# First weight block behind each norm: products with upper parts first, from a zeroed bank

## The reference, cut to what matters

```
def rms_norm(x, g):                      # first model
    y = xf * rsqrt(mean(xf * xf) + 1e-6)
    return y * g
h = rmsnorm(x, ln1_g[l]) * (1.0 + sc1) + sh1     # second model, modulated
z = h @ w_in[l]
...
h = rmsnorm(x, ln2_g[l]) * (1.0 + sc2) + sh2
f = (silu(h @ w_gate) * (h @ w_up)) @ w_down
```

## Time and profile before

| | |
|---|---|
| time, median of 3 runs | 2083.06 us (2082.49 to 2087.9) |
| the profiled execution, its own time | 2090.85 us |
| its span, first to last instruction | 2089.0 us |
| PE busy | 2033.1 us, 97% of the span, 12394 products |
| DVE busy | 1717.8 us, 82% |
| ACT busy | 1248.3 us, 60% |
| mean granted TensorE clock | 0.986 of full speed |
| up to the mixture of experts | some 1220 us of the span |

### The profile page before, as it was taken

How to read it: one execution, slowest core, us unless ns; L and a number is a source line. 1 busy time by engine, 2 the same in 40 slices (tenths; PEclk the granted TensorE clock), 3 DMA queues, 4 the chain that set the end, 5 groups by cost and what they waited for, 6 DMA issues and landing times. The chain is left out here.

```text
span 2089.0 us, 31399 instructions
## 1 busy us (share of the span) xinstructions
PE 2033.1 (97%) x12394; PEld 1760.4 (84%) x12395; DVE 1717.8 (82%) x1984; ACT 1248.3 (60%) x1258; POOL 49.0 (2%) x84
## 2 busy tenths in 40 slices
PE   9999999999899999999999999999999999999998
PEld 8889996987799989799998878888888788888876
DVE  6868887786788878778788788988898889989997
ACT  5664444542443455643345767777777777777775
POOL 0000001000000000000000000000000000000000
PEclk9999999998899999999999999999999999999999
DMA  7358861301477735388874259998999899999995
GB/s 284 126 199 287 307 231 54 112 15 48 167 279 263 259 127 181 107 307 302 302 262 147 101 198 374 355 377 327 377 349 370 322 366 359 358 352 364 358 352 207
DMA packets 79466, 534.53 MB, mean 256 GB/s; under 512 B 11840, under 2 KB 13120, under 8 KB 15584
## 3 DMA queue, kind: packets, MB, share of 16 engines
q1 hardware_dynamic: 71744, 481.04, 62.1%
q0 software_dynamic: 7440, 51.49, 6.8%
q10 hardware_dynamic: 144, 0.02, 0.0%
HBM read 531.47 MB, written 1.05 MB: 255 GB/s over the span
## 5 line engine op out<-in xcount | busy, mean ns | idle before, releaser
L2433 DVE TENSOR_TENSOR weights_lo<-ring,weights_hi 128x2048 fp32r<-128x2048 f32 x193 | 436.8, 2280 | 63.7 <-ACT weights_hi L2427 63.4
L826 PE MATMUL bank<-acts_hi,weights_hi 128*128 128x256 f32 x1584 | 454.1, 287 | 6.9 <-DVE acts_lo L425 4.3
L403 DVE TENSOR_TENSOR weights_lo<-ring,weights_hi 128x2048 fp32r<-128x2048 f32 x161 | 368.1, 2290 | 110.0 <-ACT weights_hi L393 108.9
L393 ACT CAST weights_hi<-ring 128x2048 fp32r<-128x2048 f32 x161 | 306.9, 1908 | 250.1 <-PE bank L826 224.6
L826 PE MATMUL bank<-acts_lo,weights_hi 128*128 128x256 f32 x1584 | 448.1, 283 | 0.0
L826 PE MATMUL bank<-acts_hi,weights_lo 128*128 128x256 f32 x1584 | 448.0, 283 | 0.0
L2427 ACT CAST weights_hi<-ring 128x2048 fp32r<-128x2048 f32 x192 | 367.4, 1918 | 80.5 <-PE bank L2948 49.9
L826 PEld LDWEIGHTS bank<-acts_hi,weights_hi 128*128 128x128 f32 x1584 | 303.6, 192 | 15.9 <-issue 12.9
L2948 PE MATMUL bank<-weights_hi,xg_hi 128*128 128x512 f32 x768 | 305.2, 397 | 6.7 <-issue 2.9
L826 PEld LDWEIGHTS bank<-acts_lo,weights_hi 128*128 128x128 f32 x1584 | 303.8, 192 | 2.6 <-issue 1.4
L826 PEld LDWEIGHTS bank<-acts_hi,weights_lo 128*128 128x128 f32 x1584 | 303.7, 192 | 0.0
(11 more groups left out here) (498 smaller groups left out, 2868.7 us busy)
## 6 DMA issues: line engine op xcount, KB each, us to landing
ring<-in_experts SPq DMA_DIRECT2D x192, 1024.0 KB, 6.6
ring<-in_dense SPq DMA_DIRECT2D x162, 1024.0 KB, 4.9
ring_more<-in_experts SPq DMA_DIRECT2D x96, 1024.0 KB, 6.7
ada<-in_ada POOLq DMA_DIRECT2D x48, 1024.0 KB, 5.1
silu_c<-in_c SPq DMA_DIRECT2D x3, 512.0 KB, 6.9
resid<-in_x SPq DMA_DIRECT2D x2, 512.0 KB, 4.2
out<-resid SPq DMA_DIRECT2D x4, 256.0 KB, 2.2
small<-in_consts SPq DMA_DIRECT2D x1, 649.5 KB, 10.3
```

Source lines behind the costliest of these rows:

```text
L393: nc.scalar.copy(split[0][:, n % SPLITS, :], ring[:, n % RING, :]).then_inc(hi_ready, 1)
L403: nc.vector.tensor_tensor(split[1][:, n % SPLITS, :], ring[:, n % RING, :], split[0][:, n % SPLITS, :].bitcast(F32), ALU.subtract).then_in ...
L826: ins = nc.tensor.matmul(bank[:, f * T:(f + 1) * T], split[w][:, m % SPLITS, k * 256 + f * P:k * 256 + (f + 1) * P], acts[x][:, k, :], sta ...
L2433: ins = nc.vector.tensor_tensor(split[1][:, at, lo:hi], place(j)[0][:, lo:hi], split[0][:, at, lo:hi].bitcast(F32), ALU.subtract)
```

## The change

It has four parts.

1. A new function, `to_features_upper_first`, takes the place of `to_features` for the first block at six places: gate block 0 of FFN 0, 1 and 2, the receptance block `q` = 4, and `win(0)` of both mixers. It first multiplies a piece of the table that holds zeros with 512 columns into the whole bank, which starts the sum, and then makes the same 48 products in another order: those with upper parts of a pair (8) wait for `at_hi`, those with its lower part (4) for `at_lo`, in the order upper 0, upper 1, lower 0, upper 2, lower 1, upper 3, lower 2, lower 3.
2. The block's bank is now 7 instead of 0, at the five norms, as DVE still reads banks 0 to 3 when the products begin; whoever reads the result reads bank 7.
3. In a modulated norm ACT writes the upper part of pair 0 straight from the bank, without `AT`, and makes the full value of pair 2 as well; DVE makes that of pair 3 and then that of pair 0, which only the lower part needs now.
4. The two filling products behind the transposes are left out ahead of mixer 0, FFN 2 and mixer 1.

```
             def act_columns(self, act):
-                for b in range(4 if self.direct else 2):
+                at_once = range(4) if self.direct else (0,) if self.parts else ()
+                for b in range(4 if self.direct else 3 if self.parts else 2):
                     act.wait_ge(turned, 4 * self.turns + b + 1)
...
-                        dst = acts[0] if self.direct else AT
+                        dst = acts[0] if b in at_once else AT
...
-                    for c in range(2, 4):
-                        at_round(act, self.no, c)
+                    at_round(act, self.no, 3)
...
             def dve_columns(self, dve):
                 if not self.direct:
-                    for b in range(2, 4):
+                    for b in (3, 0) if self.parts else (2, 3):
                         dve.wait_ge(turned, 4 * self.turns + b + 1)
+                        if b == 0:
+                            dve.wait_ge(at_hi, 4 * self.no + 1)
...
+                        if c == 0:
+                            dve.wait_ge(at_ready[0], self.no + 1 - skipped[0])
                         at_rest(dve, self.no, c)
...
+        def to_features_upper_first(pe, m, bank, no):
+
+            def product(f, k, w, x, stop):
+                return nc.tensor.matmul(bank[:, f * T:(f + 1) * T],
+                                        split[w][:, m % SPLITS, k * 256 + f * P:k * 256 + (f + 1) * P],
+                                        acts[x][:, k, :], start=False, stop=stop)
+
+            def upper(c):
+                pe.wait_ge(at_hi, 4 * no + c + 1)
+                for f in range(2):
+                    for k in (2 * c, 2 * c + 1):
+                        for w in range(2):
+                            product(f, k, w, 0, False)
+
+            def lower(c):
+                pe.wait_ge(at_lo, 4 * no + c + 1)
+                for f in range(2):
+                    for k in (2 * c, 2 * c + 1):
+                        ins = product(f, k, 0, 1, f + k == KT)
+                return ins
+
+            nc.tensor.matmul(bank, const("causal", P, P), const("cos", 0, 2 * T), start=True, stop=False)
+            landed(pe, m)
+            upper(0)
+            upper(1)
+            lower(0)
+            upper(2)
+            lower(1)
+            upper(3)
+            lower(2)
+            lower(3).then_inc(used, 1)
...
-                                to_features(pe, at["gate", j], pb[j % 2], None if j else no)
+                                if j:
+                                    to_features(pe, at["gate", j], pb[j % 2])
+                                else:
+                                    to_features_upper_first(pe, at["gate", 0], pb[7][:], no)
...
-                        norm.pe(pe, *((2, 3), (6, 2), (3, 2))[name])
+                        norm.pe(pe, *((2, 3), (6, 0), (3, 0))[name])
...
+                        elif q == 4:
+                            to_features_upper_first(pe, nk + q, pb[q % 4][:], numbers[1])
...
+                            if i == 0:
+                                to_features_upper_first(pe, n0, pb[7][:], no)
...
-                        norm.pe(pe, *((2, 2), (4, 1))[l])
+                        norm.pe(pe, *((2, 0), (4, 1))[l])
```

More of the change, by code:

```diff
@@ L515, in act_columns @@
                         f = 2 * b + i
-                        dst = acts[0] if self.direct else AT
+                        dst = acts[0] if b in at_once else AT
                         ins = nc.scalar.activation(dst[:, f, :], pb[b][:, i * T:(i + 1) * T], ACT.Identity,
                                                    scale=self.gain(f), bias=self.bias(f) if self.bias else 0.0)
-                    if self.direct:
+                    if b in at_once:
                         ins.then_inc(at_hi, 1)
@@ L1406, in _ @@
                             act.wait_ge(used, at["gate", j] + 1)
+                            gate_bank = pb[j % 2 if j else 7]
                             if conv is None:
@@ L1409, in _ @@
                                     act.wait_ge(hidden, hb + j - 1)
-                                nc.scalar.activation(sg[:, j % 2, :], pb[j % 2][:], ACT.Silu).then_inc(gate_copied, 1)
+                                nc.scalar.activation(sg[:, j % 2, :], gate_bank[:], ACT.Silu).then_inc(gate_copied, 1)
                             else:
@@ L1415, in _ @@
                                     act.wait_ge(gate_pads, 2 * conv + 2)
-                                nc.scalar.copy(gp[:, j % 2, :, 2:], pb[j % 2][:].rearrange("p (f t) -> p f t", f=2)).then_inc(gate_copied, 1)
+                                nc.scalar.copy(gp[:, j % 2, :, 2:], gate_bank[:].rearrange("p (f t) -> p f t", f=2)).then_inc(gate_copied, 1)
                             round_to(act, at["up", j] + 4)
@@ L1671, in _ @@
                             to_tokens(pe, nk + q, pb[q % 4])
+                        elif q == 4:
+                            to_features_upper_first(pe, nk + q, pb[q % 4][:], numbers[1])
                         else:
-                            to_features(pe, nk + q, pb[q % 4], None if q % 4 else numbers[q // 4])
+                            to_features(pe, nk + q, pb[q % 4], None if q else numbers[0])
                         if q == 5:
@@ L2501, in win @@
                                 pe.wait_ge(win_read, 10 * l + i - 1)
-                            if i >= V0:
+                            if i == 0:
+                                to_features_upper_first(pe, n0, pb[7][:], no)
+                            elif i >= V0:
                                 to_tokens(pe, n0 + i, pb[i % 2])
                             else:
-                                to_features(pe, n0 + i, pb[i % 2], None if i else no)
+                                to_features(pe, n0 + i, pb[i % 2])
                         def rotation(b):
@@ L2617, in read @@
                             act.wait_ge(used, n0 + i + 1)
-                            two = pb[i % 2][:].rearrange("p (f t) -> p f t", f=2)
+                            two = pb[i % 2 if i else 7][:].rearrange("p (f t) -> p f t", f=2)
                             if i in ROTATED:
```

## The result

| | before | changed |
|---|---|---|
| median | 2083.38 us (7 runs, 2081.98 to 2087.9) | 2094.35 us (7 runs, 2092.42 to 2098.28) |
| ratio | | 1.0045, 95% interval 1.0033 to 1.0057 |
| profiled execution | 2090.85 us | 2092.42 us |

What follows compares the result with a forecast made beforehand. PE, busy 97% of the span, was taken as the bound, its losses being waits; the places' savings sum to 6.3 us, so 2083.06 - 6.3 = 2076.8 us, range 2073.3 to 2082.0 us.

Steps and rivals of the forecast that it cites:

- Queued behind: Work after the six places: no DMA is moved, ACT's and DVE's delays vanish in waits for PE, PE's lead passes on.
- The sum of 6.3 us: Saving over all six places: 0.78 + 0.70 + 0.78 + 3 x 1.34 us.
- FFN 0 and FFN 1: Direct norms: zero product follows the transposes, then 48 products without a stop; next block 0.78 us earlier at each.
- `q` = 4: RWKV's receptance block: PE starts after ACT's first rounding; next block 0.70 us earlier.
- FFN 2: Modulated norm, worked out for mixer 0 and mixer 1 too: next block 1.34 us earlier at each.
- zero product at 0.86 us: PE's queue at each place: the added zero product costs as much as a 512-column filling product, 0.86 us.
- stop ahead of upper 1: PE at the modulated norms: a stop of 0.47 us between upper 0 and upper 1.
- Part of it is given back later: Rival, chance 0.25: lead not passed on in RWKV and both mixers, 3.4 us lost, time 2080.2 us.
- More than that: Rival, chance 0.12: modulated norms, ACT's pair takes 0.76 us and weights come in time; 2.2 us more saved, 2074.6 us.
- Slower: the clock: Rival, chance 0.05: less filling behind the transposes lowers PE's granted clock at the norms; 2087.0 us.
- Doesn't do what it says: Rival, chance 0.03: zero product as slow as the wait it replaces; direct norms give nothing, others 0.5 us each, 2081.6 us.
- 0.55: Chance of the forecast case, 5 to 7.5 us saved over the kernel, with the 0.3% line through its middle.

Runs made afterwards that it cites:

- first: Kernel before with three more instructions (fulfilled waits) on ACT ahead of the expert loop: 2103.12 us, ratio 1.0085.
- eighth: Kernel before with one more instruction on ACT ahead of the loop, which then begins at place 1006: 2098.23 us, one execution.
- tenth run: Changed kernel with one more instruction on ACT ahead of the loop, which then begins at place 1009: 2078.01 us, one execution.
- second run: Changed kernel with six more instructions (fulfilled waits) on ACT ahead of the expert loop: 2077.76 us, ratio 0.9969.
- fifth run: Kernel before with only the modulated norms (mixer 0, FFN 2, mixer 1) changed, plus the six more instructions on ACT: 2081.09 us, ratio 0.9985.

## Why the prediction was wrong

**The step that failed** is not one of the six terms but the list of what was costed. I wrote under "Queued behind": "No DMA is moved", and followed every engine for late data. From the order of the instructions I read "One rounding (L419) went, and one pair of L518 came", and counted it in time and not in places. Three more instructions on ACT stood in no term of the sum, so their price was put at nothing; they are 15.5 to 17.1 us by the profiles, and 14 to 18 us by the times of the first, eighth and tenth run. A loop that jumps back was behind all places of the change, and nothing that I asked of the trace was about its head. The earlier trace rows and the waits of before could not show it, for there the loop just fits.

**The sum of 6.3 us** was right: by the second run 6.5 us by the ratio (interval 4.2 to 8.8) and 6.0 by the medians. Its terms, from the changed kernel's profile: FFN 0 and FFN 1 0.79 each (0.78 predicted; 9.27 - 8.48 and 9.26 - 8.48), `q` = 4 0.72 (0.70; 7.31 - 6.59 us from ACT's first rounding to the next block), FFN 2 1.42 (1.34). The zero product at 0.86 us is confirmed by its doubling. ACT's new pair, of which the trace had no row, takes 1.02 us, the bound that I took. The stop ahead of upper 1 was 0.37 us by my way of counting (upper 0 leaves the queue at 880.38 + 0.12 = 880.50 us, upper 1 begins at 880.87), for my 0.47, and the profile books 0.21 of it as idle. The queue is free at 884.94 + 0.96 = 885.90 us and the weights are there at 883.63 + 2.28 = 885.91 us, as close to each other as I had them; the next block begins at 885.97 us.

**"Part of it is given back later" (0.25)** had the right sign for the loop and the wrong mechanism: no loss is seen in the mixers, where the stretches kept their gain, and in RWKV the scatter of the stretch hides 0.70 us. **"More than that" (0.12)** did not come: weights and ACT's pair took what I had said. **"Slower: the clock" (0.05)** named a real follower but the wrong place: no low clock stands at the five norms, while behind the stall at the loop's head it is 0.53. It is a share of the loss, 15.5 us or more for 6.7 + 6.2 us of idle time. **"Doesn't do what it says" (0.03)** did not come: queue, block and wait moved as written.

**The chances.** Half of 0.55 is 0.28 and not 0.29, so faster by over 0.3% should have had 0.40, and the rest 0.55. 0.05 for slower was too little since all of it hung on one mechanism. The control of the loop's place was to be had ahead: the body's length and its place in ACT's list are in the built program, and the page of the Trainium skill named above has the rule. I had looked for what speaks against this change at TensorE alone.

**What stays open.** How PE's places are counted: 8, 10 and 12 more bring a wait of 2.9 to 3.4 us, 3, 4 and 24 more and 12 fewer do not, and I have no rule for it, nor for the round in which it shows. Of the direct norms' 2.3 us alone no run showed the whole at the end of the kernel. ACT's place 1007 was not run, and 1006 and 1009 once each. That what ACT waits for at the loop's head is code is read from four packets on q14 in the time of each stall and from the fit with three bad places; the trace does not name the cause of an "issue". Which packets of q14 belong to which jump was read from their times only.

## What to carry to other kernels

Before a change to a kernel with a loop, count each engine's instructions ahead of the loop and in its body; a change that adds one instruction anywhere ahead can move the loop to a place where each jump back stalls (ACT's 1005 to 1006 here), and no term at the place of the change shows it. In the trace, look at the first row behind each jump back: several us of idle time put down to "issue", with packets on that engine's instruction queue that the other kernel doesn't have there, point at code being fetched; moving the loop by a few instructions decides it. If a good idea comes out slower, try it once more with a few fulfilled waits ahead of the loop before dropping it: here it made 1.0045 into 0.9969. Better than padding would be a body short enough to fit from any place, by the figures of the Trainium skill's page named above an estimated 257 instructions or fewer. It wasn't tried; DVE's loop of 247 instructions moved by six places without a stall, which fits.

## What was not expected of the hardware

Three waits on ACT, in code that runs once, cost 17.7 us. The executions of one kernel scatter with the mean granted clock: those of the fifth run go from 2077.2 us at 0.989 to 2085.1 us at 0.985, so that two kernels a few us apart are better compared by stretches whose clock is 1.00. And a stall in a loop costs PE more than its length, since PE goes on at a granted clock near half behind it (0.53 from 1445 to 1449 us, and 1.00 in the four us behind that): 6.69 us of idle time made that round 8.4 us longer.
